# A hybrid decoder step: the feed-forward block as seven products per slab, its hidden result through DRAM

## What is computed

```
def swiglu(xn, p):
    return (jax.nn.silu(xn @ p['ffn_w_gate']) * (xn @ p['ffn_w_up'])) @ p['ffn_w_down']
x = x + rmsnorm(m, ...)                             # mixer: RG-LRU and gated DeltaNet heads
x = x + rmsnorm(c, p['norm_xa_post'])               # memory cross-attention
f = swiglu(rmsnorm(x, p['norm_ffn_pre']), p)
x = x + rmsnorm(f, p['norm_ffn_post'])
```

## Time and profile before

| | us |
|---|---|
| median of 3 runs (lowest to highest) | 3570.13 (3569.66 to 3572.38) |
| span of the profiled execution, first to last instruction | 3571.9 |
| the profiled execution's own time | not given apart; within the runs' 2.7 us |
| mean TensorE clock over the span | 0.967 |
| TensorE, VectorE, ScalarE, GpSimd busy | 3347.2, 1395.6, 931.7, 304.2 |

### The profile page before, as it was taken

How to read it: one execution, slowest core, us unless ns; L and a number is a source line. 1 busy time by engine, 2 the same in 40 slices (tenths; PEclk the granted TensorE clock), 3 DMA queues, 4 the chain that set the end, 5 groups by cost and what they waited for, 6 DMA issues and landing times.

```text
span 3571.9 us, 62658 instructions
## 1 busy us (share of the span) xinstructions
PE 3347.2 (94%) x26460; PEld 3214.3 (90%) x26460; DVE 1395.6 (39%) x1693; ACT 931.7 (26%) x1381; POOL 304.2 (9%) x285
## 2 busy tenths in 40 slices
PE   7999999998798998898899699999999999999996
PEld 7999999996588897896299599999999999999996
DVE  4544244426757524526122733332233332233324
ACT  4432233326011223213022322221122221122212
POOL 0000000001322023101112300000000000000023
PEclk9999999998799999999899899999999999999998
DMA  7552333322200322427632233332333332333331
GB/s 251 165 171 88 92 92 94 87 56 61 71 1 0 106 89 83 149 88 266 229 133 92 89 95 93 89 94 91 92 94 88 94 94 89 94 91 91 109 122 65
DMA packets 403690, 369.59 MB, mean 103 GB/s; under 512 B 17499, under 2 KB 392556, under 8 KB 395839
## 3 DMA queue, kind: packets, MB, share of 16 engines
q1 hardware_dynamic: 394362, 295.53, 27.5%
q0 software_dynamic: 8960, 70.62, 5.2%
q10 hardware_dynamic: 272, 2.10, 0.1%
HBM read 346.21 MB, written 22.24 MB: 103 GB/s over the span
## 4 chain that ended last, share of the span: by engine, by line
PE 64%; DVE 6%; DMA 1%; ACT 1%; issue 1%; POOL 0%; DVEq 0%; ACTq 0%; POOLq 0%
PE ps L1665 56%; PE ps L1976 2%; PE ps L1805 2%; PE ps L1814 1%; DVE branch L1457 1%; PE ps L1820 1%; DMA cache<-in_cache_mem_k 1%; DVE x_low L1462 1%; DVE xt L1474 1%; DVE cache L1519 1%; DVE ssum L1444 0%; PE ps L1954 0%; DVE xt_last L1474 0%; DVE w_low L1114 0%; DVE x_low L1409 0%
## 5 line engine op out<-in xcount | busy, mean ns | idle before, releaser
L1114 DVE TENSOR_TENSOR w_low<-w_raw,w_high 128x1024 fp32r<-128x1024 f32 x524 | 644.6, 1231 | 1824.0 <-ACT w_high L733 1824.0
L1665 PE MATMUL ps<-x_high,w_high 128*128 128x260 f32 x5920 | 1195.5, 283 | 62.1 <-DVE x_low L1462 51.2
L1665 PE MATMUL ps<-x_low,w_high 128*128 128x260 f32 x5920 | 1192.1, 283 | 0.0
L1665 PE MATMUL ps<-x_high,w_low 128*128 128x260 f32 x5920 | 1189.9, 282 | 0.0
L733 ACT ACTIVATE w_high<-w_raw 128x1024 fp32r<-128x1024 f32 x524 | 554.9, 1060 | 1803.0 <-PE ps L1665 1683.7
L1665 PEld LDWEIGHTS ps<-x_high,w_high 128*128 128x128 f32 x5920 | 911.6, 189 | 71.0 <-issue 42.2
L1665 PEld LDWEIGHTS ps<-x_low,w_high 128*128 128x128 f32 x5920 | 917.3, 190 | 0.0
L1665 PEld LDWEIGHTS ps<-x_high,w_low 128*128 128x128 f32 x5920 | 915.4, 189 | 0.0
L1665 PE MATMUL ps<-h_low,w_high 128*128 128x260 f32 x1408 | 282.3, 282 | 0.0
L1665 PE MATMUL ps<-h_high,w_high 128*128 128x260 f32 x1408 | 282.1, 282 | 0.0
L1665 PE MATMUL ps<-h_high,w_low 128*128 128x260 f32 x1408 | 281.8, 281 | 0.0
(11 more groups left out here) (381 smaller groups left out, 2451.7 us busy)
## 6 DMA issues: line engine op xcount, KB each, us to landing
w_raw<-in_w_in SPq DMA_DIRECT2D x96, 512.0 KB
w_raw<-in_ffn_w_gate SPq DMA_DIRECT2D x176, 256.0 KB
w_raw<-in_ffn_w_up SPq DMA_DIRECT2D x176, 256.0 KB
w_raw<-in_ffn_w_down SPq DMA_DIRECT2D x88, 512.0 KB
w_raw<-in_xa_wk SPq DMA_DIRECT2D x32, 512.0 KB
w_raw<-in_xa_wv SPq DMA_DIRECT2D x32, 512.0 KB
w_raw<-in_w_out SPq DMA_DIRECT2D x32, 512.0 KB
w_raw<-in_xa_wq SPq DMA_DIRECT2D x32, 512.0 KB
```

The lines of the kernel that those rows point to most:

```text
L1114: dve.tensor_tensor(w_low[:, slot], w_raw[:, (g.slab0 + jj) % RAW], w_high[:, slot].bitcast(F32), ALU.subtract).then_inc(sem("w_low_ready" ...
L1665: ins = pe.matmul(ps[:, b + 2 * m + h, 0:HALF], wk, x[:, c, h * HALF:(h + 1) * HALF], **flags)
```

## The change

The block is written anew with the Winograd form of Strassen's scheme. The 2×2 structure of the weights is (two neighbouring chunks of the contraction) × (gate and up, or two neighbouring output chunks); that of the activations is (the two chunks) × (the two token halves). A slab of 4 chunks holds two such pairs.

- **TensorE** makes seven products per pair, each into its own PSUM bank, with three passes and only 260 tokens: 7 × 2 × 3 = 42 matmuls a slab. The waits for the combining steps stand inside the first slab of a unit.
- **Weights**: per slab two differences on GpSimd (one in place), two on VectorE, 256 elements each; then ScalarE copies 8×128 and 6×128 elements to `w_hi`, and VectorE subtracts them to `w_lo`.
- **Operand sets**: per pair of chunks three sums of 260 elements on GpSimd and one on VectorE, copies of 4×260 and 3×260 on ScalarE, and as many subtractions on VectorE (`set_high`, `set_low`).
- **Combining**: per unit one copy of 260 on ScalarE and four sums on VectorE (520, 260, 520, 520) that read PSUM, into `prods`.
- **Gate-up**: VectorE scales the gate half, GpSimd the up half (`scale_up`), ScalarE Silu, VectorE the product into `h_out`, and SP stores it to `h_mid` in DRAM. All 44 hidden chunks come first; then the down products in three parts of 16, 16 and 12 chunks, each reading its pairs back from `h_mid` and making sets of them while the last unit before still runs.
- **Down**: GpSimd copies (first part) or adds (others) `prods` to `ffn_out` (`gather`); in the last part ScalarE squares it and GpSimd adds the squares.
- **Second boundary in pieces of two chunks**: `post_normed` (VectorE), `pre_normed` (ScalarE, which also stores the new x piece and fetches the next old one), `set_sums` (GpSimd), `set_low_of` (VectorE). x stays in `x_mid` and comes back for the tail. Two weight slabs are converted ahead of the first piece, two between pieces.
- GpSimd's descriptor memory for its DMAs goes from the default to 4096 bytes.

The main helpers and the order in a gate-up unit, cut; in turn they are GpSimd's (with its down unit), SP's, ScalarE's, VectorE's (with its boundary loop), TensorE's, and the host's:

```diff
+            def slab_sums(m, k):
+                n = 4 * m + k
+                pool.wait_ge(sem(f"f_loaded{k}"), 32 * (m + 1))
+                if type(n) is not int or n >= 2:
+                    pool.wait_ge(sem("f_low"), n - 1)
+                a = raw[k]
+                pool.tensor_tensor(w_sums[k % 2][:, 0], a[:, :, 0, 1], a[:, :, 0, 0], ALU.subtract).then_inc(sem("f_sum3"), 1)
+                pool.wait_ge(sem("f_sum3"), n + 1)
+                pool.tensor_tensor(a[:, :, 0, 1], a[:, :, 0, 1], a[:, :, 1, 1], ALU.subtract).then_inc(sem("f_sum1"), 1)
+            def set_sums(q, src, t):
+                if q:
+                    pool.wait_ge(sem("f_set"), q)
+                pool.tensor_tensor(t[:, 0], src[:, 1], src[:, 3], ALU.add).then_inc(sem("f_t3"), 1)
+                pool.wait_ge(sem("f_t3"), q + 1)
+                pool.tensor_tensor(src[:, 1], src[:, 1], src[:, 0], ALU.subtract).then_inc(sem("f_t1"), 1)
+                pool.wait_ge(sem("f_t1"), q + 1)
+                pool.tensor_tensor(t[:, 1], src[:, 3], src[:, 1], ALU.add).then_inc(sem("f_t2"), 1)
...
+            def up_unit(u):
+                for k in (2, 3):
+                    slab_sums(u, k)
+                for k in (0, 1):
+                    slab_sums(u + 1, k)
+                scale_up(u)
...
+                def down_unit(v, p=p, m=m):
+                    for k in (2, 3):
+                        slab_sums(v + m, k)
+                    slab_sums(v + (m + 1), 0)
+                    gather(p, v)
+                    slab_sums(v + (m + 1), 1)
...
+            def up_loads(u, parity):
+                load_up(u, 0)
+                load_up(u, 1)
+                store_h(u - 2, parity)
+                load_up(u, 2)
+                load_up(u, 3)
...
+            def slab_high(m, k):
+                n = 4 * m + k
+                act.wait_ge(sem("f_sum1"), n + 1)
+                if type(n) is not int or n >= 2:
+                    act.wait_ge(sem("f_used"), n - 1)
+                act.activation(w_hi[k % 2][:, 0:8], raw[k][:].rearrange("p a b c d -> p (a b c) d"), ACT.Copy).then_inc(sem("f_high"), 1)
+                act.wait_ge(sem("f_sum4"), n + 1)
+                act.activation(w_hi[k % 2][:, 8:14], w_sums[k % 2][:].rearrange("p s k c -> p (s k) c"), ACT.Copy).then_inc(sem("f_high"), 1)
+            def up_unit(u):
+                for k in (2, 3):
+                    slab_high(u, k)
+                slab_high(u + 1, 0)
+                first_product(u)
+                slab_high(u + 1, 1)
+                gated(u)
...
+            def slab_sums(m, k):
+                n = 4 * m + k
+                dve.wait_ge(sem("f_sum1"), n + 1)
+                a, t = raw[k], w_sums[k % 2]
+                dve.tensor_tensor(t[:, 1], a[:, :, 0, 0], a[:, :, 0, 1], ALU.subtract).then_inc(sem("f_sum2"), 1)
+                dve.wait_ge(sem("f_sum2"), n + 1)
+                dve.tensor_tensor(t[:, 2], a[:, :, 1, 0], t[:, 1], ALU.subtract).then_inc(sem("f_sum4"), 1)
+            def slab_low(m, k):
+                n = 4 * m + k
+                hi, lo = w_hi[k % 2], w_lo[k % 2]
+                dve.wait_ge(sem("f_high"), 2 * n + 1)
+                dve.tensor_tensor(lo[:, 0:8], raw[k][:].rearrange("p a b c d -> p (a b c) d"), hi[:, 0:8].bitcast(F32), ALU.subtract)
+                dve.wait_ge(sem("f_high"), 2 * n + 2)
+                dve.tensor_tensor(lo[:, 8:14], w_sums[k % 2][:].rearrange("p s k c -> p (s k) c"), hi[:, 8:14].bitcast(F32),
+                                  ALU.subtract).then_inc(sem("f_low"), 1)
+            def up_unit(u, parity, count):
+                for k in (2, 3):
+                    slab_step(u, k)
+                slab_step(u + 1, 0)
+                combine(u)
+                combine_end(u, 4 * u + 4)
+                scale_gate(u)
+                slab_step(u + 1, 1)
+                hidden(u, parity, count)
+            for kp in range(KP):
+                if kp + 1 < KP:
+                    post_normed(kp + 1)
+                set_low_of(kp, kp, xn[kp % 2], t_first)
+                if kp in (3, 5):
+                    slab_sums(0, (kp + 1) // 2)
+                    slab_low(0, (kp + 1) // 2)
...
+            def products(slab_of, slots, n, sets=None, first=False):
+                for s, k in enumerate(slots):
+                    pe.wait_ge(sem("f_low"), slab_of(s) + 1)
+                    if sets is not None:
+                        pe.wait_ge(sem("f_set"), sets + 2 * s + 2)
+                    for bank, (m, x) in enumerate(PRODUCTS):
+                        if s == 0 and not first:
+                            if bank == 0:
+                                pe.wait_ge(sem("f_p1"), n)
+                            elif bank == 1:
+                                pe.wait_ge(sem("f_prod"), 4 * n - 3)
+                            elif bank >= 3:
+                                pe.wait_ge(sem("f_prod"), 4 * n - 5 + min(bank, 5))
+                        for half in range(2):
+                            kp = 2 * s + half
+                            high, low = weight(w_hi[k % 2], m, half), weight(w_lo[k % 2], m, half)
+                            pe.matmul(ps[:, bank, 0:HALF], high, set_high[:, kp, x], start=kp == 0, stop=False)
+                            pe.matmul(ps[:, bank, 0:HALF], high, set_low[:, kp, x], start=False, stop=False)
+                            ins = pe.matmul(ps[:, bank, 0:HALF], low, set_high[:, kp, x], start=False, stop=kp == 2 * len(slots) - 1)
...
-    nc = bacc.Bacc("TRN2", target_bir_lowering=False, num_devices=1)
+    nc = bacc.Bacc("TRN2", target_bir_lowering=False, num_devices=1, dynamic_dma_scratch_size=4096)
```

More of the change, by code:

```diff
@@ L1599, in _ @@
+            weigh_last(0)
+            for c in range(0, NC, 2):
+                for k in (c + 1, c + 2):
+                    if k < NC:
+                        weigh_last(k)
+                dve.wait_ge(sem("post_last"), c + 1)
+                dve.tensor_tensor(last(c), last(c), ffn_out[:, c], ALU.add).then_inc(sem("x_new_even"), 1)
         @block_.tensor
@@ new lines, in new_summed, with up_unit @@
+            def new_summed():
+                pe.wait_ge(sem("f_xsum"), NC)
+                pe.matmul(ps[:, 7, :], ones[:], xsum[:, 0:512], start=True, stop=True)
+                pe.matmul(ps[:, 6, 512 - (T - 512):512], ones[:], xsum[:, 512:T], start=True, stop=True).then_inc(sem("f_summed"), 1)
+            four = range(4)
+            products(lambda s: s, four, 0, sets=0, first=True)
+            new_summed()
+            def up_unit(u):
+                products(lambda s: 4 * u + s, four, u)
@@ L1993, in _ @@
+            pe.wait_ge(sem("f_osum"), NC)
+            pe.wait_ge(sem("f_prod"), 4 * UNITS)
+            for h in range(2):
+                ins = pe.matmul(ps[:, h, 0:HALF], ones[:], ssum[:, h * HALF:(h + 1) * HALF], start=True, stop=True)
+            ins.then_inc(sem("f_out_summed"), 1)
             for k in range(4 * (TT + 1)):
```

615 lines of the change are left out of this document (513 added, 102 removed).

## The result

The changed kernel takes 3748.97 us, the median of 4 runs (3748.86 to 3752.91), where 4 runs of the kernel before beside it gave 3571.26 (3569.66 to 3574.6): a ratio of 1.050, 95% interval 1.0487 to 1.0513. Slower, as forecast (3731, range 3595 to 3800). Its profiled execution has a span of 3751.3 us, 179.4 more than before; it is the slowest of the four.

What follows compares the result with a forecast made beforehand. VectorE and GpSimd, taking turns on a shared SBUF path, were to make TensorE wait despite fewer matmuls: +53 + 5 − 44 + 145 + 2 = +161 us, giving 3731 on the median, range 3595 to 3800.

Steps and rivals of the forecast that it cites:

- Part 6: Down products: late hand-overs behind GpSimd's gather, units of 22.9, 24.3 and 21.8 us, plus operand sets of h: +145 us.
- Parts 1 and 2: Whole block: 42 matmuls per slab for 48, 189 us to gain at most; prices per instruction, GpSimd's 256 elements at 0.75 us.
- Rival B: GpSimd's new work: short instructions cost a third of the line, 0.25 us; 212 us less, 3519; chance 0.08.
- Part 3: VectorE and GpSimd: times add up where both read SBUF, less up to 0.1 us per instruction; combining from PSUM is free.
- Rival A: VectorE and GpSimd: the turns don't bind, the engines slip past each other; 131 us less, 3600; chance 0.15.
- Part 4: Second boundary: both engines in turn, 10.2 us per pair of chunks, +53 us; unit 1 28 for 22.9, +5.
- The x pieces: Second boundary: x returning through DRAM, asked for 7 us ahead of use, costs nothing; bound 48 us.
- Part 5: 42 gate-up units: hand-over chain of 6.8 us against 5.0 stalls TensorE 1.8; 21.8 per unit for 22.86, −44 us.
- the 97: Down products: 22 pairs of h's operand sets at 4.9 us in turn, 108 us, less 11 falling into stalls already counted.
- waits for h pieces: Down products: DMA waits at x or h pieces, named as a sign that the forecast is wrong.
- Rival C: 24 down units: stalls of 2.9 to 4.3 us also lower TensorE's clock; +58 us, 3789; chance 0.13.
- Part 7: Small terms: h store and reload 0, GpSimd's smaller descriptor memory 0, the tail's combining and gather +2 us.

Runs made afterwards that it cites:

- run 8: Changed kernel with all slab sums on VectorE one slab ahead, up scaling and operand-set sums there too, gather and square sums later in GpSimd's queue: 3667.4 us.
- run 4: Changed kernel with GpSimd's slab differences cut to 2 of 128 columns inside the hardware loops, the rest of that work left out: 3677.5 us.
- run 6: Changed kernel with GpSimd's second-boundary work cut short (set sums of seven pairs 2 of 260 columns, square sums 4 of 520): 3734.6 us.
- run 2: Changed kernel with the up scaling on VectorE in place of GpSimd: 3689.3 us.
- run 9: Kernel of run 8 with both scalings behind VectorE's next slab and the gather off GpSimd (ScalarE copy or VectorE addition): 3580.3 us.
- run 12: Kernel of run 9 with h's fifth piece asked for earlier, next slab's first sums before the last combine, ScalarE's first set copy after the second sum: 3557.6 us.
- run 3: Changed kernel with both gate-up scalings behind VectorE's conversion of the next unit's second slab: 3750.7 us.
- run 5: Changed kernel with the work on h's operand sets cut to 2 of 260 columns, order, waits and DMAs kept: 3703.6 us.
- run 1: Changed kernel with GpSimd's gather behind both differences of the next unit's second slab in all down units: 3701.4 us.

## Why the prediction was right, point by point

The sum was right within 18 us of 3749, by its main mechanism in the boundary and in the up units. In the largest term, the down part, two errors of more than 50 us each nearly cancel (Part 6): there the closeness of the sum is luck.

- **Parts 1 and 2, prices.** The count held. VectorE's 0.42 and 0.96 measured 0.422 and 0.976 alone (run 8), GpSimd's 0.75 is the 0.74 of L668 where it works unheld, its addition of 1040 elements 2.42. Rival B, which needs 0.25, falls.
- **Part 3, turns.** Right for instructions that read SBUF twice: the same 256 elements take VectorE 0.88 us with GpSimd at work and 0.42 without. The step from PSUM (L2022) has a mean of 0.70 in both. Rival A falls: VectorE's means are far above the unheld ones, and fell when only GpSimd's instructions were shortened (run 4). Its price had a slip: 22 sets at 1.5 are 33, not 25, which would make it 3592. The Trainium skill (GPSIMD Engine Reference, Specifications) has the contention for VectorE instructions "in a 2-port perf mode or with two SBUF inputs"; the traces agree on both sides.
- **Part 4, the boundary.** +51.6 for +53, pairs of 10.1 for 10.2, unit 1 +6 for +5. The size was right, the reason half: it is a ring through ScalarE, too, and with GpSimd nearly gone a pair still took 8.0 (run 6), where the sum of both engines' times would have been about 6.6 (5.4 and the 1.2 put down for the shortened work). The x pieces cost one wait of 3.64 us, at the start, forecast at 0.
- **Part 5, up units.** 21.94 for 21.8: the stall is the 1.80 of the sum (run 2), TensorE's own unit 20.14 for 20.0. That the place is the hand-over is borne out by runs 2, 8, 9 and 12 together; run 3 by itself looked like the contrary.
- **Part 6, down.** The term that was mis-sized: +159 for +145. The six units around the changes of set came as forecast (233.6 for 235, which is 138 of ordinary units and the 97), and slabs there took 14 to 18 us for 14. But the text had the 97 down to turns alone, and the working failed there: with the work cut short only 49 went (run 5). The other 41 most likely are the pieces' landing, one after the other through two buffers, and the clock behind these waits. The text had put the landing at nothing beyond the 97, and had named waits for h pieces as a sign of being wrong; they came, 39.8 us in seven. The excess is in the ordinary units: 143.0 us for six in part 0 (23.8 for 22.9), 157.6 for six in part 1 (26.3 for 24.3), 150.9 for seven in part 2 (21.6 for 21.8): 5.6 + 11.8 − 1.7 = 15.7. Seen from TensorE the working is further off than the sum. From 3018.6 to 3703.7 us it was idle 156.0 us, where Part 6 with the last up unit has 1.8 + 8 × (2.9 + 4.3 + 6.8) + 97 = 210.8; but its 3874 matmuls took 529.1 us, where 119.9 ns each would be 464.5. So 55 us of waits too many stand against 65 us of slower matmuls that the term left out. It is plainest in part 2: idle 4.2 us per unit for the 6.8 counted, and 17.5 us of matmuls for 15.0, which make 21.7 for 21.8.
- **Rival C, the clock,** was true as a mechanism. In parts 0 and 1 it is the excess: the stalls are the forecast 2.9 and 4.3 within 0.2 (2.7 and 4.1 on the weight loads' rows), and 842 matmuls take 106.19 and 111.56 us at 0.96 and 0.91, where run 1, at 1.00, has 102.04: 0.8 and 1.9 per unit. Over the whole down part it is some 54 of the 65 us above. This is an estimate: at 1.00, too, a stall adds 0.27 us to TensorE's busy time (102.04 in run 1 with five stalls, 100.70 in run 12 with none), and there are some 40. So C's +58 was about right in size. The time did not come to its 3789 because the waits were 55 us shorter than counted; whether slower matmuls themselves shortened the waits wasn't separated. With the stall at 0.5 (run 1) or 1.5 once per unit (up units) the clock stayed at 1.00. The Trainium skill (TensorE: Matmul & The Clock Gate, What's actually happening) says "the default state is throttled, and activity releases the throttle"; the traces agree for the stalls of 1.9 us (run 1, part 1, at 0.93) and more, and not for those of 1.5.
- **Part 7.** The tail cost nothing, for +2.
